# State-space blocks in 64x64 tiles without zero padding, contiguous loads of C and of the skip vector, and later weights loaded during the scan

## The reference, cut to what matters

```python
mod = silu(cond) @ w_ada + b_ada                     # (6 x 1024) shift, scale, gate: two sub-layers
h = rms_norm(x) * (1 + sc1) + sh1
u = h @ w_in                                         # ssm_mixer
y = u * d_skip
for d in range(2):                                   # forward, backward
    a, bb = zoh_discretize(lam[d], log_dt[d], b[d])
    x_t = einsum("blgh,gph->blgp", u_g, bb)          # plus a * h0 at the first token
    h_t = associative_scan(h_t = a * h_{t-1} + x_t)
    y = y + Re(einsum("blgp,ghp->blgh", h_t, c[d]))
val, gate = split(gelu(y) @ w_glu)
x = x + g1 * (val * sigmoid(gate))
h = rms_norm(x) * (1 + sc2) + sh2
x = x + g2 * moe(h)                                  # router, top-2 of 16 experts, D_EXPERT = 1024
return rms_norm(x), final scan states
```

## Time and profile before

| | |
|---|---|
| median of 3 runs | 998.11 us (996.9 to 998.47) |
| span of the profiled execution | 997.0 us |
| PE busy | 800.8 us (80%) |
| DVE busy | 329.0 us (33%) |
| ACT busy | 195.6 us (20%) |
| POOL busy | 98.2 us (10%) |
| moved by DMA | 259.14 MB, mean 260 GB/s |

### The profile page before, as it was taken

How to read it: one execution, slowest core, us unless ns; L and a number is a source line. 1 busy time by engine, 2 the same in 40 slices (tenths; PEclk the granted TensorE clock), 3 DMA queues, 4 the chain that set the end, 5 groups by cost and what they waited for, 6 DMA issues and landing times.

```text
span 997.0 us, 19297 instructions
## 1 busy us (share of the span) xinstructions
PE 800.8 (80%) x7936; PEld 464.8 (47%) x7937; DVE 329.0 (33%) x894; ACT 195.6 (20%) x372; POOL 98.2 (10%) x109
## 2 busy tenths in 40 slices
PE   4158999970169999965999999999999999999750
PEld 0035668930039944534545455454553555545320
DVE  6149983699910002224021120211111121121116
ACT  0033316300230212210021120211111121121113
POOL 1020002067020010002000000000000000000000
PEclk8579999975579999986999999999999999999995
DMA  8910000440554570047999999999999999999924
GB/s 306 342 14 1 2 0 2 170 171 8 159 214 169 199 273 0 1 165 300 343 397 410 410 410 410 408 410 410 410 410 410 335 413 410 410 411 410 410 74 189
DMA packets 78154, 259.14 MB, mean 260 GB/s; under 512 B 19384, under 2 KB 19816, under 8 KB 73880
## 3 DMA queue, kind: packets, MB, share of 16 engines
q1 hardware_dynamic: 70840, 253.04, 65.0%
q10 hardware_dynamic: 5632, 2.18, 1.3%
q0 software_dynamic: 1632, 3.20, 0.9%
HBM read 252.49 MB, written 6.29 MB: 260 GB/s over the span
## 4 chain that ended last, share of the span: by engine, by line
issue 47%; DVE 3%; POOL 2%; DMA 2%; POOLq 1%; ACT 0%; SPq 0%; DVEq 0%
POOL y_scratch L495 1%; POOLq L513 1%; DMA slots<-slot_list 1%; DMA ring<-y_scratch 0%; DVE ring L1457 0%; DVE sreg L1446 0%; DVE sreg L1447 0%; POOL slot_list L469 0%; DVE sreg L1448 0%; POOL pool_tick L483 0%; DMA slot_list<-sreg,sloti 0%; DMA y_scratch<-vreg,sidx 0%; POOL sidx L488 0%; ACT sreg L723 0%; POOLq L512 0%
## 5 line engine op out<-in xcount | busy, mean ns | idle before, releaser
L995 PE MATMUL ps<-ring,vreg 128*32 128x512 f32 x2240 | 246.6, 599 | 14.1 <-issue 13.8
L995 PEld LDWEIGHTS ps<-ring,vreg 128*32 128x32 f32 x2240 | 74.6, 111 | 179.0 <-issue 179.0
L1017 PE MATMUL ps<-ring,vreg 128*32 128x256 f32 x2240 | 124.2, 380 | 17.0 <-ACT vreg L702 17.0
L1017 PEld LDWEIGHTS ps<-ring,vreg 128*32 128x32 f32 x2240 | 81.3, 110 | 56.0 <-issue 16.3
L745 PE MATMUL ps<-ring,silu_c 128*32 128x512 f32 x192 | 39.6, 925 | 72.8 <-DMA ring<-in_w_ada 72.8
L981 PEld LDWEIGHTS ps<-vreg,sreg 128*128 128x128 f32 x768 | 89.3, 196 | 14.2 <-issue 12.6
L981 PE MATMUL ps<-vreg,sreg 128*128 128x96 f32 x768 | 91.9, 281 | 1.5 <-DVE vreg L1378 1.5
L1408 DVE TENSOR_TENSOR vreg<-vreg,ps 128x256 f32<-128x256 f32 x48 | 17.4, 417 | 224.3 <-ACT vreg L697 224.3
L1418 DVE COPY vreg<-ps 32x256 f32<-32x256 f32 x96 | 40.7, 424 | 132.2 <-PE ps L1017 129.7
L954 PE MATMUL ps<-ring 128*128 128x512 f32 x192 | 83.1, 593 | 0.7 <-ACT ring L652 0.7
L709 ACT ACTIVATE vreg<-ps 32x256 f32<-32x256 f32 x96 | 35.9, 374 | 131.5 <-PE ps L1017 129.5
(11 more groups left out here) (257 smaller groups left out, 682.2 us busy)
## 6 DMA issues: line engine op xcount, KB each, us to landing
ring<-in_moe_w_gate SPq DMA_DIRECT2D x128, 512.0 KB, 11.8
ring<-in_moe_w_up SPq DMA_DIRECT2D x128, 512.0 KB, 13.2
ring<-in_moe_w_down SPq DMA_DIRECT2D x128, 512.0 KB
ring<-in_w_ada SPq DMA_DIRECT2D x24, 1024.0 KB, 8.8
ring<-in_ssm_w_glu SPq DMA_DIRECT2D x8, 1024.0 KB, 4.8
ring<-in_ssm_w_in SPq DMA_DIRECT2D x8, 512.0 KB, 12.5
ring<-y_scratch SPq DMA_DIRECT2D x6, 512.0 KB, 6.2
tmat<-ada_rows SPq DMA_DIRECT2D x4, 512.0 KB, 7.1
```

What stands on the lines that cost most here:

```text
L995: last = pe.matmul(ps[t][32 * j:32 * j + 32, :], xgT[:, k, 32 * t:32 * t + 32], w[:, :, 256 * j:256 * j + 256], start=(k == 0), stop=(k == ...
L1017: last = pe.matmul(ps[3 + t // 2][32 * dj:32 * dj + 32, 256 * (t % 2):256 * (t % 2) + 256], aT[:, t, c2, 32 * j:32 * j + 32], ring[:, KT + ...
```

## The change

Three kinds of edit, in words:

1. `pt` is 64 columns per group instead of 128x128 blocks with zeros; L853 becomes two 64x64 matmuls (K = 64, M = 64) on the two diagonal quadrants, both into the same PSUM bank. `y_state` reads `V` itself with the same two quadrants; `v_pad` with its ACT copies, and all of POOL's zeroing, go. `store_W` copies both groups with one 128-partition instruction, from four banks used in turn instead of two pairs.
2. C comes in two contiguous loads, and PE transposes it in 64-column halves; `ssm_d` comes in one load of 8 rows (`drow`), two small PE transposes and one ACT copy make `dtab`; the skip term is added by 16 matmuls at the end of each bank of within-chunk kernels, so POOL's addition goes. `kpad` moves to slot 0.
3. The late pieces of `w_ada` pass through slots 4 to 7 and start when the input product is done; `w_glu` takes slots 8 to 11 when L853's successor is done, and 4 to 7 behind the last pieces of `w_ada`; `load_T` moves from SP to ACT; the wait before `w_in` goes.

```diff
-        kpad = ring[:, 7, 0:16 * 112].rearrange(...)
+        kpad = ring[:, 0, 0:16 * 112].rearrange(...)
-        pads = ring[:, 4:12, :]...
-        pt = [pads[:, (1 - d) * 2 * GP:(2 - d) * 2 * GP, :]... for d in range(2)]
-        v_pad = pads.rearrange("p (g d r) j -> p g d r j", d=2, r=2)
+        pt = ring[:, 8:12, :]...rearrange("p (d g r s) -> p d g r s", d=2, g=GP, r=2)
@@ sync
-            sp.wait_ge(ld_ada[6], 16)
             for k in range(KT):
                 sp.dma_start(win[:, k, :], w_in[0, k * P:(k + 1) * P, :]).then_inc(ld_win, 16)
...
-            sp.wait_ge(pe_p, 16)
+            sp.wait_ge(pe_u, 8)
             for n in range(KT, 3 * KT):
                 b, k = divmod(n, KT)
-                if n == KT + 8:
-                    load_T()
+                if n == KT + 4:
+                    sp.wait_ge(pe_p, 32)
+                    for kk in range(4, KT):
+                        load_glu(kk)
                 if n >= KT + 4:
                     sp.wait_ge(pe_ada, n - 3)
-                sp.dma_start(ring[:, 8 + n % 4, :],
+                sp.dma_start(ring[:, 4 + n % 4, :],
                              w_ada[0, k * P:(k + 1) * P, b * UNIT:(b + 1) * UNIT]).then_inc(ld_late[n % 4], 16)
+            for k in range(4):
+                sp.wait_ge(pe_ada, 2 * KT + k + 5)
+                load_glu(k)
@@ gpsimd
-            zero_blocks(2 * GP, 4 * GP, 0)
...
-            pool.tensor_tensor(kpad[:, :, :, 48:64], kpad[:, :, :, 48:64], dskip[:, :, :, :], ALU.add
-                               ).then_inc(pool_k, 1)
@@ scalar
+            act.dma_start(drow[:, 0:P], ssm_d[0].rearrange("(m p) -> m p", p=P)).then_inc(ld_drow, 16)
...
-                for i in range(2):
-                    act.dma_start(cnat[r * DG:(r + 1) * DG, :].rearrange("p (h i s) -> p i h s", h=GS, i=2)[:, i],
-                                  cc.rearrange("a d (g i) h s -> i (a d g) h s", i=2)[i]).then_inc(ld_bc, 16)
-            for q in range(4):
-                for i in range(2):
-                    act.dma_start(dtab[32 * q:32 * q + 16, i, :], ssm_d[0]...[q, i],
-                                  allow_slow_non_contiguous=True).then_inc(ld_dtab, 16)
+                act.dma_start(cnat[r * DG:(r + 1) * DG, :], cc.rearrange("a d (g i) h s -> (a d g) (i h s)", i=2)
+                              ).then_inc(ld_bc, 16)
...
-                    for i in range(2):
-                        a = slice(64 * i, 64 * i + 64)
-                        act.activation(pt[d][a, g0:g0 + 8, r, a], ps[2 * (w % 2) + i][a, :]..., ACT.Copy)
+                    act.activation(pt[:, d, g0:g0 + 8, r, :], ps[w % 4][:, :]..., ACT.Copy)
...
-            for half in range(2):
...
-                        act.activation(v_pad[a, g, d, :, a], V[...], ACT.Copy).then_inc(act_vpad, 1)
+            act.wait_ge(act_k, 4)
+            for i in range(2):
+                for j in range(L):
+                    for q in range(4):
+                        act.dma_start(tmat[...], kpad[...]).then_inc(ld_tmat, 16)
@@ tensor
-                        last = pe.matmul(ps[m % 8][:, o:o + CX], pt[d][:, g0 + gi, r, :], uT[:, g0 + gi, :],
-                                         start=True, stop=True)
+                        for i in range(2):
+                            a = slice(64 * i, 64 * i + 64)
+                            last = pe.matmul(ps[m % 8][a, o:o + CX], pt[a, d, g0 + gi, r, :], uT[a, g0 + gi, :],
+                                             start=True, stop=True)
...
+                    for q in range(4):
+                        a = slice(32 * q, 32 * q + 32)
+                        last = pe.matmul(bank[32 * q:32 * q + 16, 0:448]...[:, :, 48:64], i16[a, :],
+                                         dskip[a, i, 4 * mq:4 * mq + 4, :], start=False, stop=True,
+                                         skip_group_check=True)
...
-                            last = pe.matmul(ps[k][:, q * CX:(q + 1) * CX], v_pad[:, 4 * k + q, d, r, :],
-                                             S[:, d, d:d + CX, r, 4 * k + q], ...)
+                            for i in range(2):
+                                a = slice(64 * i, 64 * i + 64)
+                                v = V[a, d * GP + 4 * k + q, r, 1 - d:5 - d, :].rearrange("p k h -> p (k h)")
+                                last = pe.matmul(ps[k][a, q * CX:(q + 1) * CX], v, S[a, d, d:d + CX, r, 4 * k + q], ...)
...
             pe.wait_ge(dve_scan, 1)
-            pe.wait_ge(act_vpad, 8)
-            pe.wait_ge(pool_pad, 8)
```

More of the change, by code:

```diff
@@ L167, in build @@
         scr = cut(vreg, D)
+        drow = cut(vreg, P + GS)[0:8, :]
         off[0] = 2 * DG * NP_V * GS - NT * D
@@ L319, in _ @@
             sp.wait_ge(st_rows, 32)
-            for k in range(KT):
-                sp.wait_ge(pe_y, k + 1)
-                sp.dma_start(ring[:, 4 + k, :], w_glu[0, k * P:(k + 1) * P, :]).then_inc(ld_glu, 16)
+            sp.wait_ge(pe_y, KT)
             for cond in range(2):
@@ L632, in _ @@
                                ACT.Copy).then_inc(act_k, 1)
[L634 to L645 removed]
+            act.wait_ge(act_k, 4)
+            for i in range(2):
+                for j in range(L):
+                    for q in range(4):
+                        dst = tmat[64 * i + 16 * j:64 * i + 16 * j + 16, q:GP:4, :]
+                        act.dma_start(dst, kpad[32 * q:32 * q + 16, i, :, (3 - j) * GS:(7 - j) * GS]
+                                      ).then_inc(ld_tmat, 16)
             def store_yT(k):
@@ L755, in _ @@
             pe.transpose(ps[3][:, 0:16], rows[0:16, :], ident[0:16, 0:16]).then_inc(pe_tr, 1)
+            pe.wait_ge(ld_drow, 16)
+            pe.wait_ge(pool_zero, 4)
+            for i in range(2):
+                pe.transpose(ps[5][:, 8 * i:8 * i + 8], drow[:, GS * i:GS * i + P], ident[0:8, 0:8])
             pe.wait_ge(ld_lam, 16 * 5)
@@ L872, in _ @@
                                                      skip_group_check=True)
+                    for q in range(4):
+                        a = slice(32 * q, 32 * q + 32)
+                        last = pe.matmul(bank[32 * q:32 * q + 16, 0:448].rearrange("p (m w) -> p m w", w=112)[:, :, 48:64],
+                                         i16[a, :], dskip[a, i, 4 * mq:4 * mq + 4, :], start=False, stop=True,
+                                         skip_group_check=True)
                     last.then_inc(pe_k, 1)
```

99 lines of the change are left out of this document (33 added, 66 removed).

## The result

The changed kernel takes **967.7 us** (median of 4 runs, 964.67 to 969.72) against 998.3 us for the kernel before, run beside it: a ratio of 0.968 [0.966, 0.971]. It is faster, but 18.7 us above the forecast of 949 and outside its range. The profiled execution spans 965.8 us, 31.2 less than before, where 49.0 less was forecast.

A forecast was written before the change was run, and what follows sets the result against it. The kernel was taken as a row of stages with different limits, ahead of an untouched block from L954. Terms -20.8 - 3.4 - 4.8 - 20.0 = -49.0 us gave a 948.0 us span, 949 us forecast; range 936 to 960 us.

The forecast's parts named there:

- Step 1: Head: contiguous loads let w_ada's piece 7 land at 34 to 35.6 us, modulation rows added 20.8 us earlier.
- The near tie with the squares: Head: ACT's squares of the tokens end at 35 to 37 us, rows are added between 36.2 and 37.7.
- Steps 2 and 3: Tables: transpose_W without waits for ACT's copies, -3.4 us; L853 as 512 half-size instructions at L879's pace, -4.8 us.
- Step 4: After the scan: y_state waits for no late pieces, POOL addition or v_pad copies, -20.0 us; loads hidden beside the scan.
- Rival D: Head and after the scan: loads not hidden or head not freed, half of either or both gains lost; 959 to 969 us; 8 in 100.
- Step 5: y_state (L857): 512 instructions for 256 still take 44.7 us, a pair costing 175 ns as before; no change.
- Rivals A: L815 and y_state: row tiles sharing a bank take turns, so slower, 1018 to 1027 us; 4 in 100.
- B: As a rival: only stepped reads take turns, so L853 gains but y_state costs 89.6 us; 994 us; 6 in 100.
- C: As a rival: the step costs less for half arrays, y_state takes 37.4 us; 942 us; 10 in 100 for under 942.
- the middle case: y_state: moving-side step sets the price and two quadrants run side by side, a pair 175 ns; between -20.7 and +44.7 us.
- The premise: From the GLU product (L954) to the end: untouched, starts as a block, so only its earlier start counts; no change inside.

The follow-up runs named there:

- the last two experiments on L857: Changed kernel with L815 and L857 doing one diagonal quadrant, then the other: 1004.9 us; changed kernel with L857 reading adjacent columns of uT, states left out: 946.4 us.
- 121 idle instructions: Changed kernel with 121 instructions that do nothing ahead of PE's wait for tmat: 955.3 us, ratio 0.955 to the kernel before.
- the 121 and the other edits together: Changed kernel, B and C behind w_ada's last piece, later weights held for the small DMAs, 121 idle instructions ahead of the fifth late piece: 942.4 us, 0.945.
- T ahead of the weights: Changed kernel with 12 late w_ada pieces and half of w_glu held until the 32 small DMAs have landed: 964.9 us, ratio 0.965.

## Why the prediction was wrong, and where it was right

The direction was right, and so were most stages; the sum missed by 17.8 us of span, in these terms:

| term of the prediction | forecast | measured | what was off |
|---|---|---|---|
| 1 head | -20.8 | -12.1 | rate of the 64-partition loads |
| 2 and 3 tables, L815 | -8.2 | -12.8 | L815 at 42 ns, and more |
| scan | 0 | -0.4 | |
| 4 after the scan | -20.0 | -16.9 | T issued beside the weights |
| 5 `y_state` | 0 | -2.1 | started warm |
| from L866 to GLU | 0 | +1.0 | gap of 2.30 us |
| "everything from L954 to the end is untouched and starts, as a block" | 0 | +12.1 | place of PE's code |

- **Step 1 failed** at "the rate is 426 GB/s before C's short runs come and 380 beside them. The other 5.9 MB take 14 us at 426 and 15.6 at 380". It counted bytes, and took short runs for the only reason of a lower rate. Its two rows leave out the ten microseconds between them, in which the kernel before moved 298 GB/s (there C's short runs ran too, so that row alone could not have told the two causes apart). The loads into 64 partitions, contiguous as they are, run at about half rate (202 GB/s alone) and pull the stream beside them down (to 255 and 232). The near tie with the squares came out as described, but both arms were late, since the tokens queued in the same pit. Put behind piece 7, the loads give rows at 36.54, inside the 36.2 to 37.7 of the forecast.
- **Steps 2 and 3** were right in sign, and gave 4.6 us more than forecast. L815 was forecast at 24.0 us by L879's row and took 21.64, 7.2 us less than before instead of 4.8. The reason given, "with no time shared, a pair could not take 94 ns", is wrong: one quadrant at a time costs 25.4 us, so that two in a row take 100 ns. Its conclusion, that the shared bank costs nothing, stands, but by L857's rows and not by L879's. `transpose_W` and the input product gained 5.8 us instead of 3.4. ACT's copies had cost PE 2.1 us there, not 3.4 (the 0.43 was the wait of one half batch); another 1.7 us came because one input product, 8.89 us before, now ran at full clock in 7.20; the rest was not tried apart.
- **Step 4 failed** at "and even at twice that to 222". The issue took 2.6 times SP's 20.70 us, from 190.7 to 243, and `tmat` had landed at 248 instead of 222: more than the "over 20 us to spare". The 20.70 was the price with no stream beside it. Rival D had named the mechanism, 32 DMAs among 12 MB of weights, and priced it in halves of terms; measured, it cost 3.1 us here. That the time falls into D's range (959 to 969 us) is luck: D's two parts cost 8.7 and 3.1 us, most of which steps 2, 3 and 5 gave back, and the rest is the tail, which no rival had.
- **Step 5** held: 43.0 us. Rivals A, B and C are out, and the middle case stands for its stated reason, which the last two experiments on L857 show: the step sets the price of a read, and the quadrants share the time. The 2.1 us on top are luck: it started at a clock of 1.00 and not of 0.50, since `y_inside`, late with T, ran right ahead of it and paid for the low clock (6.54 us instead of 4.25).
- **The premise failed**, and cost the most: 12.1 us. That code which isn't edited starts "as a block" and takes what it took is true of its data, not of its instructions. The change makes PE's straight program 290 matmuls longer and so moves the experts' loop against the 16 KB blocks. 10.6 of the 12.1 us lie in the three experts of the table, 1.7 in GLU; 121 idle instructions bring back 10.4 in these three. For the 6 us of the branch the cause is shown. For the 3 us of the last expert and the 1.7 in GLU it is not: with the 121 and the other edits together the last expert takes 60.5 us and not 59.4, and GLU is short with B and C moved alone as well.

## What to carry to other kernels

Before a load is costed by its bytes, look at how many partitions it fills: here those that filled half of them brought the rate of all that was queued with them from over 400 down to some 250 GB/s, so put such a load behind what is awaited (9 us for moving four lines). The 32 small DMAs took 2.5 times as long to issue beside the weight stream; hold the stream until they are out. When an edit changes the length of an engine's program ahead of a loop with branches, compare the longest time of each branch row before and after: a stall put down to "issue" with a 6 us COMPARE_BRANCH in it, and instruction packets at the same moment, can be the place of the code, and here some idle instructions where the engine waits anyway took it away.

## What the runs showed that had not been expected

- The first taking of one branch of PE costs 0.22 us or 6.0 to 7.0 us, by nothing but where the code lies; with the low clock after it, it makes 7.6 us of a kernel's time. A version comparison of under 1% can be this and nothing else.
- The granted clock fell to 0.50, the level of 1.2 GHz, without an idle PE: with one quadrant at a time it was 1.00 at 262 to 264 and 0.50 from 266 on, PE busy in every stretch. The instructions of L857 kept their pace at either level; the 128x128 ones of the kernel before, with the same step, did not (167 and 213 ns).
- Stepped reads: 64x64 instructions with 97 columns 512 bytes apart cost 152 ns on average one quadrant at a time and 84 in turn; with adjacent columns 50 and 42 to 43.
- In the changed kernel L833's last two banks run at 0.50 (6.0 and 7.1 us instead of 4.2) behind a 0.70 us gap of PE. With B and C behind the last piece the gap is as long (0.74 us) and the clock stays at 1.00, 4.4 and 4.2 us; so the gap alone does not decide it. With T ahead of the weights, and so no stream beside L833, there was no gap. Whether the stream delayed the fetch of code there was not tried apart.
